# Squared-ReLU feed-forwards in four groups, with the second weight matrix multiplied by seven block products

## The reference

```python
def _sq_relu_mlp(h, w1, w2):
    return jnp.square(jax.nn.relu(h @ w1)) @ w2
...
        h = _layer_norm(DEEPNORM_ALPHA * h + _sq_relu_mlp(h, ffn_w1[layer], ffn_w2[layer]),
                        ln_g[layer, 1], ln_b[layer, 1])
```

## Time and profile before

| what | value |
|---|---|
| median of three runs | 2663.25 us |
| profiled execution: span from the first to the last instruction | 2656.4 us |
| TensorE busy | 2615.0 us, 98% |
| VectorE, ScalarE, GpSimd busy | 63%, 48%, 7% |
| granted TensorE clock, mean | 0.998 |
| layer 0, `seven0a` to the last product of `down0b` | 332.6 us |
| layer 1, the same | 320.4 us |

### The profile page before, as it was taken

How to read it: one execution, slowest core, us unless ns; L and a number is a source line. 1 busy time by engine, 2 the same in 40 slices (tenths; PEclk the granted TensorE clock), 3 DMA queues, 4 the chain that set the end, 5 groups by cost and what they waited for, 6 DMA issues and landing times.

```text
span 2656.4 us, 42476 instructions
## 1 busy us (share of the span) xinstructions
PE 2615.0 (98%) x16497; PEld 2236.1 (84%) x16497; DVE 1675.5 (63%) x2902; ACT 1268.0 (48%) x2049; POOL 183.4 (7%) x234
## 2 busy tenths in 40 slices
PE   9999999999999999999999999999999999999998
PEld 9877799999999798779898786766877777799996
DVE  4544586264565465487265535875589987696784
ACT  4556365153454354365154434254365564475561
POOL 1111000000000000100000012051000000000000
PEclk9999999999999999999999999999999999999999
DMA  9994936858556564736557979922433333254451
GB/s 355 222 230 119 216 92 234 207 165 248 135 171 212 146 184 140 232 110 196 145 164 245 260 187 266 253 66 80 145 94 114 119 111 120 81 189 148 156 174 56
DMA packets 187722, 450.56 MB, mean 170 GB/s; under 512 B 14984, under 2 KB 31368, under 8 KB 186896
## 3 DMA queue, kind: packets, MB, share of 16 engines
q1 hardware_dynamic: 108368, 264.29, 29.4%
q0 software_dynamic: 60000, 167.78, 26.7%
q10 hardware_dynamic: 19168, 15.93, 2.0%
HBM read 438.24 MB, written 159.51 MB: 225 GB/s over the span
## 4 chain that ended last, share of the span: by engine, by line
PE 85%; DVE 8%; ACT 4%; issue 2%; DMA 0%; POOL 0%; DVEq 0%; ACTq 0%; POOLq 0%
PE ps L399 29%; PE ps L1546 25%; PE ps L549 6%; PE ps L3344 4%; PE ps L2354 2%; PE ps L1991 2%; PE ps L2145 2%; PE ps L2029 2%; PE ps L2891 2%; PE ps L791 2%; PE ps L919 2%; DVE w_lo L370 1%; PE ps L878 1%; ACT w_hi L362 1%; DVE xs L3044 1%
## 5 line engine op out<-in xcount | busy, mean ns | idle before, releaser
L370 DVE TENSOR_TENSOR w_lo<-raw,w_hi 128x1024 fp32r<-128x1024 f32 x500 | 611.1, 1223 | 467.1 <-ACT w_hi L362 466.1
L362 ACT ACTIVATE w_hi<-raw 128x1024 fp32r<-128x1024 f32 x500 | 527.1, 1055 | 512.9 <-PE ps L399 292.3
L1546 PE MATMUL ps<-x_hi,w_hi 128*128 128x264 f32 (+1 forms) x1120 | 317.4, 283 | 2.1 <-DVE rg L1925 0.7
L1546 PE MATMUL ps<-x_hi,w_lo 128*128 128x264 f32 (+1 forms) x1120 | 316.3, 282 | 0.0
L1546 PE MATMUL ps<-x_lo,w_hi 128*128 128x264 f32 (+1 forms) x1120 | 316.1, 282 | 0.0
L399 PE MATMUL ps<-x_hi,w_hi 128*128 128x512 f32 (+1 forms) x688 | 248.3, 378 | 4.4 <-DVE x_lo L1410 2.7
L399 PE MATMUL ps<-x_lo,w_hi 128*128 128x512 f32 (+1 forms) x688 | 244.3, 372 | 0.0
L399 PE MATMUL ps<-x_hi,w_lo 128*128 128x512 f32 (+1 forms) x688 | 243.2, 371 | 0.0
L1546 PEld LDWEIGHTS ps<-x_hi,w_hi 128*128 128x128 f32 x1120 | 210.8, 188 | 5.0 <-issue 2.2
L1546 PEld LDWEIGHTS ps<-x_hi,w_lo 128*128 128x128 f32 x1120 | 211.1, 188 | 0.0
L1546 PEld LDWEIGHTS ps<-x_lo,w_hi 128*128 128x128 f32 x1120 | 210.6, 188 | 0.4
(11 more groups left out here) (503 smaller groups left out, 5827.8 us busy)
## 6 DMA issues: line engine op xcount, KB each, us to landing
raw<-in_weights SPq DMA_DIRECT2D x255, 512.0 KB
raw<-weight_sums SPq DMA_DIRECT2D x280, 256.0 KB
weight_sums<-in_weights POOLq DMA_DIRECT2D x36, 1536.0 KB, 19.4
raw<-in_weights SPq DMA_DIRECT2D x210, 256.0 KB
weight_sums<-in_weights POOLq DMA_DIRECT2D x12, 2048.0 KB, 31.1
weight_sums<-in_weights POOLq DMA_DIRECT2D x12, 1792.0 KB, 22.1
weight_sums<-weight_sums POOLq DMA_DIRECT2D x12, 1536.0 KB, 14.3
weight_sums<-weight_sums POOLq DMA_DIRECT2D x4, 2048.0 KB, 19.7
```

Of the source, the lines that this page charges most:

```text
L362: nc.scalar.activation(w_hi[:, s], raw[:, s], ACT.Copy).then_inc(hi_ready, 1)
L370: nc.vector.tensor_tensor(w_lo[:, s], raw[:, s], w_hi[:, s], ALU.subtract).then_inc(lo_ready, 1)
L1546: last = nc.tensor.matmul(out_, w[:, s, 4 * (b % 2) + k], a, start=kind in "125" and k == n == 0, stop=k == 3 and n == 2, skip_group_check ...
```

## The change

Each feed-forward is done in four groups of 8 hidden tiles instead of two of 16. In every group the product with `w2` is made by seven block products as well (28 block products of four tiles for 4 pairs of output tiles, 336 matmuls), from 12 whole and 4 half chunks that are split. The sums it needs aren't made in DRAM: the plain blocks of `w2` are loaded into the ring and into three buffers beside it (`odd_at`), and GpSimd adds them in SBUF (`block_sum`, 8 per group, two instructions each, 512 or 1024 columns). The activation sums are also GpSimd's (`pair_turns`, for each pair of hidden tiles three or four instructions, of 528 or 264 columns), and so are the four sums for the up stages (`turn_sum_pool`, in place of `turn_sum`). VectorE's squares are made in place. In the down stages ScalarE copies the results of 1, 5 and 6, and VectorE adds copies and PSUM quarters to `x32`, 28 additions of 264 (256) columns per group in place of 8 additions of 528 (512) columns per down stage. Of the layer norm behind it, four subtractions and three additions go from VectorE to GpSimd (`aid_pool`). The DMAs of the later stages' weight sums are spread one step at a time between GpSimd's additions.

The core of the diff (helpers that only count semaphores are left out; `POOL_MADE` counts GpSimd's instructions in its program order):

```diff
-STAGES += [("up0a", 4), ("seven0a", 21), ("down0a", 16), ("seven0b", 28), ("down0b", 16)]
+STAGES += [("up0a", 4), ("seven0a", 7), ("down0a", 16)]
+for _q in "bcd":
+    STAGES += [(f"seven0{_q}", 14), (f"down0{_q}", 16)]
...
-KGROUPS = {n: 2 for n in ("down0a", "down0b", "down1a", "down1b")}
...
+DOWN_ORDER = [(b[0], int(b[1])) for b in ("10 11 20 21 50 51 60 61 70 30 71 40 12 31 22 41 52 13 62 23 72 53 32 63 42 73 33 43").split()]
+DOWN_CHUNKS = ["1" + i for i in "01"] + ["5" + i for i in "01"] + "70 40 71 12 41 52 13 72 53 42 73 43".split()
+DOWN_SUMS = ["50", "51", "70", "71", "52", "72", "53", "73"]
...
+        def stream_down(sp, name):
+
+            g0 = FIRST_CHUNK[name]
+
+            def even(i):
+                src = weights[FIRST_SOURCE[name] + 2 * i]
+                sp.dma_start(raw[:, (g0 + i % 2) % RING].rearrange("p k n -> p (k n)"), src).then_inc(landed[(g0 + i % 2) % RING], 16)
+
+            def odd(i):
+                src = weights[FIRST_SOURCE[name] + 2 * i + 1]
+                sp.dma_start(odd_at[name][i % 3].rearrange("p k n -> p (k n)"), src).then_inc(side_in[i % 3], 16)
+            sp.wait_ge(lo_ready, g0 - 3)
+            even(0)
+            odd(0)
+            sp.wait_ge(lo_ready, g0 - 2)
+            even(1)
+            odd(1)
+            if name[5] == "d":
+                sp.wait_ge(chunk_done, g0)
+            odd(2)
+            sp.wait_ge(lo_ready, g0 + down_chunk("1", 0) + 1)
+            sp.wait_ge(pool_made, summed_at(name, "70"))
+            even(2)
+            sp.wait_ge(pool_made, summed_at(name, "71"))
+            even(3)
+            sp.wait_ge(lo_ready, g0 + down_chunk("4", 0) + 1)
+            odd(3)
+            sp.wait_ge(pool_made, summed_at(name, "73"))
...
+            def pair_turns(self, pool, q, p):
+                plain = q == 0 and p < 2
+                pool.wait_ge(mlp_squared, self.squared(q, p))
+                second = 1 if p < 3 else 2
+                if p < 3:
+                    first, second_half, first_half = (self.h_raw[:, p, a:a + 3:2, 0:self.w] for a in (4, 3, 1))
+                    nc.gpsimd.tensor_tensor(first, second_half, first_half, ALU.subtract).then_inc(pool_made, 1)
+                else:
+                    nc.gpsimd.tensor_tensor(self.piece(self.h_raw, p, 4, 5), self.piece(self.h_raw, p, 3, 4), self.made(p, 1, 2),
+                                            ALU.subtract).then_inc(pool_made, 1)
+                    nc.gpsimd.tensor_tensor(self.piece(self.h_raw, p, 6, 7), self.piece(self.h_raw, p, 5, 6), self.piece(self.h_raw, p, 3, 4),
+                                            ALU.subtract).then_inc(pool_made, 1)
+                pool.wait_ge(pool_made, self.turned(q, p, 0))
+                nc.gpsimd.tensor_tensor(self.piece(self.h_raw, p, 2, 3), self.piece(self.h_raw, p, 5, 6), self.piece(self.h_raw, p, 4, 5),
+                                        ALU.subtract).then_inc(pool_made, 1)
+                if not plain:
+                    pool.wait_ge(seven_kept, self.fourth_squared(q, p))
+                pool.wait_ge(pool_made, self.turned(q, p, second))
+                nc.gpsimd.tensor_tensor(self.piece(self.h_raw, p, 3, 4), self.made(p, 0, 1), self.piece(self.h_raw, p, 2, 3),
+                                        ALU.subtract).then_inc(pool_made, 1)
+
+            def block_sum(self, pool, name, n):
+                kind, i = DOWN_SUMS[n][0], int(DOWN_SUMS[n][1])
+                g0, q = FIRST_CHUNK[name], "abcd".index(name[5])
+                to = raw[:, (g0 + 2 + n % 2) % RING]
+                even, odd = raw[:, (g0 + i % 2) % RING], odd_at[name][i % 3]
+                pool.wait_ge(lo_ready, g0 - 1 + n if n < 2 else g0 + DOWN_CHUNKS.index(DOWN_SUMS[n - 2]) + 1)
+                pool.wait_ge(side_in[i % 3], odd_landed(name, i))
+                if kind == "5":
+                    nc.gpsimd.tensor_tensor(to[:, 0:4], odd[:, 0:4], odd[:, 4:8], ALU.add).then_inc(pool_made, 1)
+                    pool.wait_ge(landed[(g0 + i % 2) % RING], EVEN_LANDED[name, i])
+                    pool.wait_ge(pool_made, POOL_MADE["sum", self.layer, q, n, 0])
+                    nc.gpsimd.tensor_tensor(to[:, 4:8], to[:, 0:4], even[:, 0:4], ALU.subtract).then_inc(pool_made, 1)
+                else:
+                    pool.wait_ge(landed[(g0 + i % 2) % RING], EVEN_LANDED[name, i])
+                    nc.gpsimd.tensor_tensor(to, even, odd, ALU.subtract).then_inc(pool_made, 1)
+                    pool.wait_ge(pool_made, POOL_MADE["sum", self.layer, q, n, 0])
+                    nc.gpsimd.tensor_tensor(to[:, 4:8], to[:, 4:8], to[:, 0:4], ALU.add).then_inc(pool_made, 1)
+
+            def pool(self, pool, norm, next_norm, parts):
+                for n in range(4):
+                    self.turn_sum_pool(pool, norm, n)
+                for q, hn in enumerate("abcd"):
+                    name = f"down{self.layer}{hn}"
+                    if q:
+                        part, group = parts[2 * q - 1]
+                        part(pool, group)
+                    for p in range(3):
+                        self.pair_turns(pool, q, p)
+                    for n in range(2):
+                        self.block_sum(pool, name, n)
+                    self.pair_turns(pool, q, 3)
+                    for n in range(2, 4):
+                        self.block_sum(pool, name, n)
+                    part, group = parts[2 * q]
+                    part(pool, group)
+                    for n in range(4, 8):
+                        self.block_sum(pool, name, n)
+                next_norm.aid_pool(pool)
...
+                    if b == end - 2:
+                        act.wait_ge(mlp_squared, self.squared(q, 3, "2"))
+                        self.part_hi(act, 3, 1, 2)
+                        self.pair_hi(act, q, 2)
...
+            def down_act(self, act, q, norm):
+                name = f"down{self.layer}{'abcd'[q]}"
+                begun, last = down_counts(name, "summed"), SEVEN[f"seven{self.layer}{'abcd'[q]}"] - 1
+                act.wait_ge(pool_made, self.turned(q, 3, 2))
+                self.part_hi(act, 3, 4, 7)
+                split_hi(act, Step(FIRST_CHUNK[name] + AHEAD))
+                act.wait_ge(seven_summed, seven_counts(f"seven{self.layer}{'abcd'[q]}", "273")["3", last])
...
+                    if e == 0:
+                        act.wait_ge(pool_made, self.turned(q, 3))
+                        self.part_hi(act, 3, 2, 4)
+                    c = down_ends(e)
+                    if c is not None and c < 14:
+                        split_hi(act, Step(FIRST_CHUNK[name] + c + 4))
...
+                def begin(kind, i):
+                    x = self.target(kind, i)
+                    dve.wait_ge(seven_kept, kept_[kind, i])
+                    nc.vector.scalar_tensor_tensor(x, x, factor, self.down_copy(q, kind, i), ALU.mult, ALU.add).then_inc(seven_summed, 1)
+                def add(kind, i):
+                    x, bank_ = self.target(kind, i), self.down_bank(q, kind, i)
+                    self.down_block_done(dve, name, kind, i)
+                    if kind == "4":
+                        nc.vector.scalar_tensor_tensor(x, x, factor, bank_, ALU.mult, ALU.add).then_inc(seven_summed, 1)
+                    dve.wait_ge(seven_summed, summed[{"2": "1", "7": "5", "3": "6"}[kind], i])
+                    nc.vector.tensor_tensor(x, x, bank_, ALU.add).then_inc(seven_summed, 1)
...
+        DOWN_PIECES = [("1", 0, 0, 4), ("1", 1, 0, 4), ("2", 0, 0, 3), ("2", 1, 0, 3), ("5", 0, 0, 3),
+                       ("2", 0, 3, 4), ("2", 1, 3, 4), ("5", 0, 3, 4)] + [(kind, i, 0, 4) for kind, i in DOWN_ORDER[5:]]
...
+            def aid_pool(self, pool):
+                c = slice(self.c0, T)
+                pool.wait_ge(ln_copied, 3 * self.nl + 1)
+                for j in range(self.aided):
+                    nc.gpsimd.tensor_tensor(self.xc[:, j, c], x32[:, j, c], self.shift[:, c], ALU.subtract).then_inc(pool_made, 1)
+                total = self.sq_sum[:, c]
+                for j in range(1, self.aided):
+                    pool.wait_ge(ln_squared, KT * self.nl + j + 1)
+                    if j > 1:
+                        pool.wait_ge(*self.summed(j - 1))
+                    nc.gpsimd.tensor_tensor(total, self.sq[:, 0, c] if j == 1 else total, self.sq[:, j % 3, c], ALU.add).then_inc(pool_made, 1)
...
-            for h, name in ((2, "down0a"), (3, "down0b")):
-                pool.wait_ge(chunk_done, FIRST_CHUNK[name])
-                for part in SUM_PARTS:
-                    part(pool, 1 + h)
+            mlp0.pool(pool, ln00, ln01, [(sums_copy, 3), (sums_of_two, 3), (sums_of_three, 3), (sums_of_four, 3),
+                                         (sums_copy, 4), (sums_of_two, 4), (sums_of_three, 4)])
```

735 lines of the change are left out of this document (498 added, 237 removed).

## The result

The changed kernel took **2864.39 us** in the median (2862.69 to 2868.89, four runs), the one before 2663.27 us (2659.40 to 2664.36, four runs): a ratio of **1.0768**, 95% interval 1.0756 to 1.0781. It is 201.1 us slower, where 16.8 us faster were forecast, and 178 us over the upper end of the range.

The account below looks back on a forecast made before the run. TensorE, busy 2615.0 of 2656.4 us, was taken to bound the kernel. Matmul savings of -42.8, stalls of +24.0 and smaller edits of +2 gave -16.8 us, so 2646.4 us, range 2619 to 2686.

Parts of the forecast that it names:

- 3.0 us of new stall per group: Down stages, block 70 or 71: GpSimd's instructions waiting for VectorE cost 3.7 us less 0.7 slack; eight groups, 24.0 us.
- The path at block 70: Start of each down stage: GpSimd's chain ends sum 70 at +8.7 us, split at +11.0, TensorE wants it at 11.7.
- the row of 1.22 beside the stopped 1.71: Attention trace: VectorE's split kept 1.22 us while GpSimd's addition took 1.71; read as nearest to only streaming parts excluding each other.
- later sums come out of the slack that the stall gives: Down stages: sums after blocks 70 and 71 add no further stall; the last undisturbed at about +29 us.
- The bound of 87.8 us a group: VectorE 63.3 plus GpSimd 36.5, overlapping only in 12.0 us of PSUM work: 6.0 us over TensorE's 81.8.
- 99.8 without even that overlap: Per group: VectorE's and GpSimd's work with no overlap at all, 99.8 us against TensorE's 81.8.
- Rival B: Down stages, last turns to sum 73: shared SBUF access becomes the bound, 6 to 10 us a group, 2670 to 2702; chance 0.24.
- SyncE is held by the same sums, with twelve us of slack.: Next stage's loads: the last sum frees the ring at about +29 us, twelve before that stage's first block.
- A step that waits for an earlier one's landing holds the turns behind it: GpSimd's queue with DMA issues: such delays are hidden by ten blocks of slack in `seven0b` to `seven0d`.
- The norms +2: Layer norm, work moved to GpSimd and additions behind VectorE's last subtraction: 1 us for each of two norms, 0 to 5.
- The hidden parts have under 1 us of slack: Pair 3's hidden parts, for blocks 50 and 60: under 1 us of slack, running late in the same stretch, not beside it.
- the first term of the sum: Down stages: fewer or smaller matmuls save TensorE 23.4 us in layer 0 and 19.4 in layer 1, together 42.8 us.

Follow-up runs that it names:

- e11: Changed kernel with all its sums, but the transfers GpSimd starts inside the feed-forwards for the up stages' weight sums cut to one pair: 2823.59 us, +163.9 over before.
- e1: Changed kernel with GpSimd's weight-block sums cut to two columns and each activation sum replaced by one memset: 2701.91 us, +37.7 over before.
- e5: As e1, with the up stages' weight-sum transfers that GpSimd starts cut to one pair, plain blocks read instead: 2659.78 us, +1.8 over before.
- e7: Changed kernel with each GpSimd block sum replaced by a series of memsets of its output, 2.04 us for 1024 columns: 2707.03 us, +49.0 over before.

## Why the prediction was wrong

**The balance.** The two causes can be switched off one by one:

```
                        transfers as they are   transfers small
GpSimd's sums           +201.1                  +163.9  (e11)
without them             +37.7  (e1)              +1.8  (e5)
```

GpSimd's sums cost 163 us in one column and 162 in the other, the transfers 37 and 36. Of the 163, the lock is 152 by e7, and the other 11 are the chain's own length (at 85% of it, so the lock may be a little less). What remains, +1.8 instead of -42.8, is 45 us that neither has.

**The step that failed: "3.0 us of new stall per group", as the whole price of the two engines' meeting.** It was 20.4 (163 / 8), seven times that. The mechanism was right, and the section on how the two disturb each other found it; the price followed it along one path only. Three things in the sum were wrong.

- The path at block 70 came nearly as forecast. Sum 70 ended 11.1 to 11.3 us after the start of down0b, down0c and down0d (13.3 in down0a) against "+8.7", and TensorE's waits for `w_lo` in layer 0 are 9.8 us, 2.5 a group. But that was GpSimd's side, 11 instructions that each wait 0.34 us. VectorE's side had no term, since the trace had no split that waited and the row of 1.22 beside the stopped 1.71 was read as the nearer one. It only showed who had come first. VectorE's instructions also wait, up to 2.2 us each, and TensorE waits for VectorE and not for GpSimd: 27.6 us for `x`, 18.2 for `h_raw` and 9.2 for `h_lo` in the same layer, where the sum had nothing. And "later sums come out of the slack that the stall gives" didn't hold: sum 73 ended at +41.0 to +45.6 instead of +29.
- An average isn't the price. The bound of 87.8 us a group, with only VectorE's work on PSUM overlapped, was a good one: in e11 VectorE or GpSimd is busy in 88.1 of the 101.65 us of seven0b and down0b (48.97 + 52.68), and in 89.4 of the 106.94 of seven0c and down0c (47.62 + 59.32), what overlaps counted once. The other 13.5 and 17.5 us both stand idle, for another engine or for loads. These chains had a term for block 70 alone. The group's length lies near "99.8 without even that overlap", but by chance: that overlap does happen (27 of 96 additions wholly inside one of GpSimd's).
- The clock had no term. In layer 0, e11 against e5 (412.4 against 326.6 us) is 86 us for the sums: 55 are TensorE idle, 31 are longer matmuls, with a granted clock of 0.87 to 0.97 in e11's four stages above and 1.00 in e5's. There a stall cost about half as much again behind it.

**Rival B** named the place, the sign and the mechanism, and its price was too small: 6 to 10 us a group instead of 20. It counted one pass of both engines through a down stage, 50.9 us. That is what they are busy in e11 (50.0 us in down0b, 51.1 in down0c, what overlaps counted once). down0b lasts 52.68, but down0c 59.32, and the seven stages have 48 to 49 where B left 40.9: the turns of the pairs, which GpSimd makes there, and the waits on the way into the next stage weren't in it. The Trainium skill's page SBUF — State Buffer, section Who interferes with whom, was weighed and given too little. It says that a VectorE instruction with two SBUF inputs contends with a GpSimd instruction that reads SBUF, but not with one that only writes it, and that whoever comes later blocks for the whole instruction. Here each part of it has its row: 3.15 us beside a sum, 1.62 behind a copy, 0.98 beside memsets, and never over 0.43 where one input is PSUM.

**"SyncE is held by the same sums, with twelve us of slack."** The slack was eaten by late sums (sum 73 at +41 and later, in a stage that was to last 40.9), and nothing had been said of what the DMA engines carry when the loads are sent: the transfers that GpSimd has just started. Before, the same transfers ran within down stages of 93 us, which need a chunk every 5.8 us (93.43 / 16); now they lie over the starts of seven stages, which need one every 2.9 (40.9 / 14) and whose loads have only just been allowed to start. "A step that waits for an earlier one's landing holds the turns behind it" looked at GpSimd's queue and not at the bytes. 36 us.

**The smaller edits.** "The norms +2": e5 has, at two norms, 4.6 us for ScalarE's copy, 3.4 and 2.3 and 2.2 behind the norm's sums, and 3.2 more for `x_lo` than before; so some 16 us instead of 2, and over the 10 of the two norms' upper ends. "The hidden parts have under 1 us of slack": in e5 they are up to 1.4 us late at the eight starts, 10.0 us in all. Together with 5.1 us behind VectorE's additions and 3.5 in the seven stages this makes 34 us, which is what TensorE is idle more than before (75.1 us against 41.4). The other 11 of the 45 are in the first term of the sum: TensorE's busy time fell by 32.1 us (2615.0 to 2582.9 in e5), and not by 42.8. In layer 0 it fell by 20.2 instead of 23.4. Where the rest of the shortfall lies isn't known.

**What held.** Three quarters of TensorE's saving (32.1 of 42.8). The seven stage: without stalls it is 41.07 us long. The three engines' own times, undisturbed: GpSimd's 2.39 for 1024 columns, VectorE's 1.22 and 0.69. "If stalls stand in the seven stages and at each new stage's first chunk too, B": they do.

**What wasn't tried.** The sums could be made by adding DMAs in DRAM, as for the up stages. In e1 the DMA engines are full over parts of these stages already, so I expect nothing of it, but that is argued and not shown. No version run beats the kernel before: even with both causes gone, and the sums with them, the change only comes level.

## What to carry to other kernels

If two engines take turns at something, price the waits of both sides, and leave one out only for a row that shows it not waiting when it comes second. Then follow the delay to everything that the bottleneck engine waits for, not only along the tightest chain. An engine that looks 7% busy is no free place for work that reads SBUF when VectorE splits and adds from SBUF next to it; work that only writes, or VectorE's work from PSUM, didn't mind here. And when stages get shorter, see what the background transfers are doing at each new boundary, since they keep their length.

## What the runs showed of the hardware beyond what was expected

- VectorE and GpSimd wait out each other's whole instruction, both ways: a 1024-column split took up to 3.41 us instead of 1.22, a 512-column step by GpSimd 2.01 us in the median instead of 1.29. The one that starts second waits; GpSimd's 1024-column steps, which started first, kept their 2.39.
- A GpSimd copy locks VectorE out as a sum does, a memset doesn't: the 792-column part took 0.98 us within 2.04 us of memsets.
- The price isn't linear in the time held: copies half as long as the sums cost 25 us, the sums 152 (both over e7; 36 and 163 over e1).
- About a third of the stalls' price was slower matmuls at a lower granted clock: 31 of 86 us in layer 0.
